# Output norm of a differential attention: squares moved from ScalarE to VectorE, its tail moved from PSUM to SBUF, and the head schedule of the x stream shifted by one step

## The reference, cut to what matters

```
a = p[:, 0] - lam * p[:, 1]                       # two softmaxes per head
o = einsum("bhqk,bkhe->bqhe", a, v)               # 4 heads x 128 values
o = rmsnorm(o, subln_g) * (1 - lam_init)          # over the 128 values
yc = o.reshape(..., DA_W) @ w_c_out               # 512 -> 1024
merged = g0 * ya + g1 * yb + g2 * yc + g3 * yd    # g = sigmoid of a projection
x = x + mx[5] * (merged @ w_o)
```

## Time and profile before

| what | value |
|---|---|
| median of 3 runs (3914.34 to 3919.41) | 3915.17 us |
| the profiled execution's own time | 3919.41 us |
| span of its instructions | 3917.6 us |
| mean granted TensorE clock | 0.980 |
| busy share PE, PEld, DVE, ACT, POOL | 96%, 91%, 41%, 48%, 67% |
| chain that ended last, by engine | PE 57%, issue 27%, POOL 12%, DVE 2%, ACT 2% |

### The profile page before, as it was taken

How to read it: one execution, slowest core, us unless ns; L and a number is a source line. 1 busy time by engine, 2 the same in 40 slices (tenths; PEclk the granted TensorE clock), 3 DMA queues, 4 the chain that set the end, 5 groups by cost and what they waited for, 6 DMA issues and landing times.

```text
span 3917.6 us, 93412 instructions
## 1 busy us (share of the span) xinstructions
PE 3742.7 (96%) x36101; PEld 3555.8 (91%) x36101; DVE 1617.2 (41%) x3472; ACT 1880.0 (48%) x2744; POOL 2632.6 (67%) x1186
## 2 busy tenths in 40 slices
PE   8998997998899789899999999999999999999998
PEld 7678997998699767799999999999999999999998
DVE  6544315325532554444222375763223222266442
ACT  4325446543554332354555555455555555555643
POOL 5005873885278510188888878768888889886886
PEclk9999999999999889999999999999999999999999
DMA  6554662665256535466666656646666666664664
GB/s 185 194 194 139 183 174 76 175 191 130 60 160 191 149 114 180 152 196 195 193 189 185 185 157 180 173 135 197 184 190 191 188 192 195 185 197 128 186 179 140
DMA packets 1162953, 664.96 MB, mean 170 GB/s; under 512 B 30157, under 2 KB 1122201, under 8 KB 1162551
## 3 DMA queue, kind: packets, MB, share of 16 engines
q1 hardware_dynamic: 1162679, 661.06, 57.3%
HBM read 659.92 MB, written 1.05 MB: 169 GB/s over the span
## 4 chain that ended last, share of the span: by engine, by line
PE 57%; issue 27%; POOL 12%; DVE 2%; ACT 2%; POOLq 0%; DMA 0%; DVEq 0%; SPq 0%; ACTq 0%
PE bank L861 55%; POOL wlo L621 12%; PE bank L840 1%; DVE bank L3024 1%; PE bank L1062 0%; ACT L1938 0%; ACT whi L631 0%; ACT L1946 0%; DMA raw<-in_w_in 0%; ACT W L1938 0%; PE bank L961 0%; POOLq L620 0%; ACT W L1935 0%; ACT W L1932 0%; ACT W L1946 0%
## 5 line engine op out<-in xcount | busy, mean ns | idle before, releaser
L621 POOL TENSOR_TENSOR wlo<-raw,whi 128x1024 fp32r<-128x1024 f32 (+3 forms) x1182 | 2632.4, 2245 | 1261.1 <-ACT whi L631 1255.9
L631 ACT ACTIVATE whi<-raw 128x1024 fp32r<-128x1024 f32 (+3 forms) x1182 | 1171.2, 996 | 1092.6 <-PE bank L861 902.0
L861 PE MATMUL bank<-AH,whi 128*128 128x256 f32 (+1 forms) x5712 | 1601.7, 280 | 25.2 <-DVE AL L771 9.3
L861 PE MATMUL bank<-AL,whi 128*128 128x256 f32 x5712 | 1594.3, 279 | 0.0
L861 PE MATMUL bank<-AH,wlo 128*128 128x256 f32 (+1 forms) x5712 | 1593.3, 279 | 0.0
L861 PEld LDWEIGHTS bank<-AH,whi 128*128 128x128 f32 x5712 | 1082.6, 190 | 34.2 <-issue 22.0
L861 PEld LDWEIGHTS bank<-AH,wlo 128*128 128x128 f32 x5712 | 1080.9, 189 | 0.0
L861 PEld LDWEIGHTS bank<-AL,whi 128*128 128x128 f32 x5712 | 1079.0, 189 | 0.6
L861 PE MATMUL bank<-HH,whi 128*128 128x256 f32 x1936 | 539.0, 278 | 0.0
L861 PE MATMUL bank<-HH,wlo 128*128 128x256 f32 x1936 | 536.9, 277 | 0.0
L861 PE MATMUL bank<-HL,whi 128*128 128x256 f32 x1936 | 536.9, 277 | 0.0
(11 more groups left out here) (448 smaller groups left out, 4919.0 us busy)
## 6 DMA issues: line engine op xcount, KB each, us to landing
raw<-in_ffn_w SPq DMA_DIRECT2D x420, 512.0 KB, 4.0
raw<-in_w_in SPq DMA_DIRECT2D x182, 512.0 KB, 3.9
raw<-in_ffn_w_gu SPq DMA_DIRECT2D x176, 512.0 KB, 3.8
ada_raw<-in_w_ada SPq DMA_DIRECT2D x96, 512.0 KB, 5.8
raw<-in_ffn_w_down SPq DMA_DIRECT2D x64, 512.0 KB, 4.1
raw<-in_rw_w_rkv SPq DMA_DIRECT2D x48, 512.0 KB, 4.1
raw<-in_w_ada SPq DMA_DIRECT2D x48, 512.0 KB, 5.3
raw<-in_ffn_w SPq DMA_DIRECT2D x56, 384.0 KB, 3.5
```

The costliest lines, as they stand in the source:

```text
L621: pool.tensor_tensor(wlo[slot][:, 0:n], raw[slot][:, 0:n], whi[slot][:, 0:n], ALU.subtract).then_inc(lo_ready, 1)
L631: act.activation(whi[slot][:, 0:n], raw[slot][:, 0:n], ACT.Copy).then_inc(hi_ready, 1)
L861: mm = pe.matmul(ps[:, 0:o.shape[2]], w, o[:, k0 + c, :], start=tile not in started and c == n == 0, stop=last_panel and c == nk - 1 and n ...
```

## The change

Three things. The square of `DO` is made by DVE instead of ACT, at the same step. Ln writes to SBUF (`rstd`, the upper half of `W[6]`), one Exp of 128x1024 works there in place of two of 128x512 in PSUM, and DVE's tail becomes three instructions of 128x1024 with all operands in SBUF in place of six of 128x512 with an operand in PSUM. And on the x stream all units come one step later (first scores at step 3, `last` = 20). `split` is the helper with L937 (cast) and L939 (subtract).

```diff
         def unit_steps(s):
-            at = [2 + 2 * u for u in range(NU)]
+            first = 3 if s == "x" else 2
+            at = [first + 2 * u for u in range(NU)]
...
                     if i == last + 1:                       # PE
                         pe.wait_ge(da_exp, after(pe, da_exp))
                         pe.wait_ge(da_stored, after(pe, da_stored))
-                        pe.wait_ge(da_squared, after(pe, da_squared))
+                        pe.wait_ge(head_in, after(pe, head_in))
...
-                    if i == last:                           # ACT
-                        act.wait_ge(da_stored, after(act, da_stored, NU))
-                        act.activation(W[6][:, 0:4 * S], DO, ACT.Square).then_inc(da_squared, 1)
                     if i == last + 1:
+                        rstd = W[6][:, 4 * S:8 * S]
                         for k in range(2):
                             act.wait_ge(da_sums, after(act, da_sums))
-                            act.activation(bank[5 + k][:, :], bank[5 + k][:, :], ACT.Ln,
+                            act.activation(rstd[:, 2 * k * S:2 * (k + 1) * S], bank[5 + k][:, :], ACT.Ln,
                                            bias=eps[:, 0:1], scale=1.0 / P).then_inc(act_step, 1)
-                        for k in range(2):
-                            act.wait_ge(act_step, after(act, act_step))
-                            act.activation(bank[5 + k][:, :], bank[5 + k][:, :], ACT.Exp, scale=-0.5).then_inc(root_ready, 1)
+                        act.wait_ge(act_step, after(act, act_step, 2))
+                        act.activation(rstd, rstd, ACT.Exp, scale=-0.5).then_inc(root_ready, 1)
...
-            out_hi, out_lo = branch_parts("c")              # DVE
+            t, rstd = W[6][:, 0:4 * S], W[6][:, 4 * S:8 * S]
...
+                    if i == last:
+                        dve.tensor_tensor(t, DO, DO, ALU.mult).then_inc(head_in, 1)
+                        dve.wait_ge(head_in, after(dve, head_in))
                     if i == last + 2:
-                        for k in range(2):
-                            dve.wait_ge(root_ready, after(dve, root_ready))
-                            ps, cs = bank[5 + k][:, :], slice(2 * k, 2 * k + 2)
-                            p3 = ps.rearrange("p (c t) -> p c t", t=S)
-                            dve.scalar_tensor_tensor(ps, DO[:, 2 * k * S:2 * (k + 1) * S], LAM[:, 7:8], ps,
-                                                     ALU.mult, ALU.mult).then_inc(dve_step, 1)
-                            dve.wait_ge(dve_step, after(dve, dve_step))
-                            dve.tensor_copy(out_hi[:, cs], p3).then_inc(dve_step, 1)
-                            dve.wait_ge(dve_step, after(dve, dve_step))
-                            op = dve.tensor_tensor(out_lo[:, cs], p3, out_hi[:, cs], ALU.subtract)
-                        op.then_inc(operand_ready, 1)
-                        dve.wait_ge(operand_ready, after(dve, operand_ready))
+                        dve.wait_ge(root_ready, after(dve, root_ready))
+                        dve.scalar_tensor_tensor(DO, DO, LAM[:, 7:8], rstd, ALU.mult, ALU.mult).then_inc(dve_step, 1)
+                        dve.wait_ge(dve_step, after(dve, dve_step))
+                        split(dve, DO, branch_parts("c"))
```

More of the change, by code:

```diff
@@ L432, in build @@
         da_sums = sem("da_sums")
-        da_squared = sem("da_squared")
         da_banks = sem("da_banks")
```

## The result

| what | before | after |
|---|---|---|
| median of 4 runs each, side by side | 3917.29 us (3914.34 to 3923.44) | 3957.84 us (3949.72 to 3960.8) |
| ratio after/before, 95% interval | | 1.0092 [1.0072, 1.0112] |
| the profiled execution's own time | 3919.41 us | 3942.3 us |
| its span | 3917.6 us | 3940.5 us |
| its mean granted clock | 0.980 | 0.977 |

The prediction said slower, 3942 us, in a range of 3921 to 3949. The sign is right, and so is the mechanism of the costs, but the median of 3957.84 lies 9 us above the range. The 26.5 us of the sum would be a ratio of 1.0068. The interval of the second timing contains it, that of the first does not; the second median, 3948.48, lies just inside the range. Three more executions belong to the first timing, that of the profile (3942.3), 3945.57 and 3951.95: the median of all seven is 3951.95, 3 us above the range, and they spread over 18 us.

The account below looks back on a forecast made before the run. PE, busy 96% of the span, was taken to bound the kernel. Terms 4.4 (`mix0c` tail), 14.2 (x tails), 2.8 (later start) and 5.1 (clock) gave 26.5 us, on 3915.17 making 3942 us, range 3921 to 3949.

Parts of the forecast that it names:

- What bounds the kernel: Whole kernel: PE is busy 96% of the span, so other engines' edits count only by PE's idle time.
- rival A: DVE's SBUF instructions and POOL's take turns, each waiting for the other's whole instruction: 3942 us, chance 0.57.
- Rival C: No turns, DVE's SBUF work runs beside POOL or in its idle time: +6.2 us, 3921, chance 0.12.
- The tail in `mix0c`: End of `mix0c`: DVE's three instructions alternate with POOL's, delaying PE's `cout` by 4.4 us, bounds 0 and 4.4.
- The x tails: Ends of both x stages, one step later: PE loses 8.1 us each, 14.2 together less two waits of 1.0.
- The 0.8 at the sums: On x, DVE's square ends behind POOL's subtraction: PE waits 0.8 us, counted within the tail's loss.
- B: DVE comes first in the x tails: 3937 us, or 3932 with no low clock, chance 0.2.
- D: Not slower, the later start on x pays by removing waits: -3.8 us, 3911, chance 0.08.
- The square in `mix0c`: DVE and POOL instructions meet about 0.05 us apart: cost taken as 0, upper bound 1.6 us.
- The first turn on x: Step 5 on x: PE waits 1.7 us where it waited 0.32, 1.4 more, twice, 2.8 us.
- The clock: Behind the three tail waits of 4.4 to 8.1 us, low clock loses 1.7 us each, 5.1 together.
- How the numbers follow: Time and range: 3942 from turns, lower end 3921 from no turns, upper 3949 from the local terms' upper bounds.

Follow-up runs that it names:

- second timing: The changed kernel and the kernel before timed again, 10 runs after and 31 before: 3948.48 us against 3918.5 us, ratio 1.0062.
- e5: The changed kernel with POOL's subtraction cut to the first eighth of each panel in dout and cout, output differs: 3933.03 us, ratio 1.0034.
- e10: The kernel before with the root in SBUF, the product written to PSUM, cast and subtraction left there, six instructions: 3939.7 us.
- e4: The kernel before with only the tail moved to SBUF, one Exp and three DVE instructions of 128x1024: 3952.42 us, ratio 1.0045.
- e9: The kernel before with the tail in SBUF but in six DVE instructions of 128x512: 3963.83 us.
- second trace: Profile of the changed kernel run once more, unedited: span 3952.4 us, timed at 3948.48 us, ratio 1.0062.
- e2: The kernel before with nothing but the later start of the units on x: 3952.2 us, ratio 1.0037.
- e6: The changed kernel with `conf_gate` at step 2 on x in place of step 3: 3948.74 us, ratio 1.0071.

## Why the direction was right and the size was not

**What bounds the kernel: right.** Every cost found is idle time or lost clock of PE. 14 us more of DVE's busy time (1617.2 to 1631.4) matter only where PE waits.

**Turns between DVE and POOL (rival A): right, nearly to the row.** In `mix0c` the ends were forecast at 2407.60, 2409.44 and 2412.93 and came at 2407.86, 2409.56 and 2412.86; `cout` at 2414.05 and came at 2413.98. The gaps of 0.55 and 1.09 behind POOL's end came as 0.55 and 1.08. The forecast started the multiplication 0.10 behind POOL and it started so. The Trainium skill ("SBUF — State Buffer", Who interferes with whom) says that a DVE instruction with two SBUF inputs and a GpSimd instruction that reads SBUF exclude each other. The traces agree, e5 with 1.44 against 3.37 us and e10 with 0.69 against 1.72 above all, and they add that here, with work waiting on both engines, the two alternate one instruction each. Rival C (no turns) falls with e4 and e9.

**The tail in `mix0c`: right.** 4.4 and 1.7 for the clock were forecast, 6.1; the local cost was 5.6, and 6.5 in the second trace.

**The x tails: right.** 8.1 with 1.7 for the clock and less the 1.0 won back is 8.8 for each; the local costs were 8.5 and 8.6, then 8.4 and 9.6. The 0.8 at the sums came as 0.77. What the shift contributes was too small (2.7 us without turns; e5 shows 3.3 and e2 4.1 to 4.4), but it hardly mattered beside the turns. B, with DVE first, was not seen: in both x stages of both traces PE waited over 7.1 us. D, where the shift pays, falls with e2, which won nothing and lost 15.1 us.

**The square in `mix0c`: right.** Hidden, at 1.22 us.

**The first turn on x: right in cause, too small.** A wait of 1.7 was forecast and 2.18 and 2.21 came. Behind the second the clock fell too, which the prediction had not charged. In place of 1.4 each, 1.8 and 3.3 were lost, and 3.4 and 3.2 in the second trace: 2.3 to 3.8 us above the 2.8 of the sum. e6 shows that it was the place of `conf_gate`.

**The clock: right in kind, too small.** Three stretches of low clock were charged at 1.7. But short waits can pull the clock down too. In the changed kernel run again, this is what lies around a wait of 1.95 us at the first turn (PE, the columns as above):

```profile
2572.90:2576.30 3.40, 1.45 (x12) 1.00 0.14 42
2576.50:2579.90 3.40, 3.40 (x17) 0.50 0.67 195
2579.90:2583.30 3.40, 3.40 (x31) 1.00 0.67 193
```

17 matmuls in place of 31. The same wait in the first trace (2.18 us) had no such stretch behind it. Over the eight first turns of the four traces with the later start and the old `conf_gate` it fell behind four (waits of 1.95, 2.03, 2.09 and 2.21 us) and not behind the other four (2.00, 2.03, 2.06 and 2.18). So at that length the clock is a chance, not a term. Behind the waits of 3.3 us and more ahead of `cout` it is a term, but not of one length: 3.4, 6.8 or 10.2 us, part of it while PE still waits. In e2 it was 6.8 us, around the end of the wait of 4.36:

```profile
2666.70:2670.10 3.40, 2.10 (x10) 0.50 0.83 236
2670.10:2673.50 3.40, 3.40 (x18) 0.50 0.56 155
```

**The step that failed: "How the numbers follow".** The local terms add up to 27.8 and 31.1 us in the two traces against 26.5 forecast, and on the prediction's own base 3915.17 + 31.1 = 3946.3 would still be inside the range. What was put at nothing is the spread that the kernel has without any edit: whole stages run at one of two paces, which by the table moved the two traces of the changed kernel some 11 us apart, and the traces of all the kernels here by -12.5 to +16.7 us against that of before. I read 3914.34 to 3919.41 as the spread and took the median of three runs as the time to within a few us. Beside later kernels 28 runs of the kernel before, on one chip, spread from 3922.99 to 3949.77, and 31, on another, from 3902.96 to 3936.36. The base of 3915.17 and the upper end of 3949, made from the bounds of the local terms alone, should each have carried this.

Of the 40.6 us between the first two medians (36 by the ratio), some 28 to 31 are the edit, as both traces show; between the medians of all seven executions and of before lie 34.7. In the second timing the medians lie 30.0 apart, 24 by the ratio. That the remaining 4 to 13 us of the first timing are slow stages in those executions fits the pace table and the second timing, but only one of the seven has a trace; this part is argued, not shown. What sets the pace was not found. That the sum of 26.5 came close to 27.8 is luck in part: the tails cost 22.7 where 23.7 was forecast, the first turns 5.1 where it was 2.8.

No version here beats the kernel before. All that PE waits there for POOL and for the mixes is 6.2 us, less than a measurement can tell.

## What to carry to other kernels

Moving DVE operands from PSUM to SBUF halves the number of instructions and can still be slower. Where GpSimd works on SBUF throughout, as here, each DVE instruction with two SBUF inputs, and each cast from SBUF to SBUF, waited for the whole GpSimd instruction under way (3.37 us against 1.44, 1923 ns against 692); an input in PSUM freed it, and cutting the work in pieces made it worse. Before moving a block of work by one step, look at what the queue of each engine holds at the new step, and at how far the last operand is from the matmul that wants it: one step was 3.5 us of cover here, and all of it was in use. And give a range the spread that a kernel has by itself, from many executions or from the pace of PE in the trace, before adding the terms of the edit.

## What the runs showed of the hardware that was not expected

PE has two paces at the same granted clock of 1.00: 885 or 851 matmuls of 128x256 in 100 us, changing between stages and between executions of one kernel. The DMA rate goes with it (191 to 194 GB/s against 183 to 185). PE frees the slots that the loads fill, so the rate can be the effect of the pace; whether it is that or its cause is open.

The granted clock fell to 0.50 behind short waits in some executions and not in others: behind 1.44, 1.95 and 2.21 us, and not behind 2.18. The shortest is in a place that no edit touches, a wait for DVE (`AL`, L771 in the kernel before) near the end that takes 1.23 to 1.24 us in every trace: the clock fell behind it in 8 of the 12 traces, that of before among them (at 3716.0 us, for 3.4 us, after 3.4 us in which PE was busy for 1.59). Behind the 25 waits of 3.3 to 7.7 us ahead of `cout` in these traces it fell each time: for 3.4 or 6.8 us around waits of 3.3 to 4.4, for 6.8 or 10.2 around those of 7.1 and more.
